# The order of TensorE's work in the first attention of a two-block kernel: pairs of heads taken two at a time

## The reference, cut to what matters

```python
s = einsum('bgrqd,bgkd->bgrqk', qb, kb) - slopes * dist      # 8 heads of 64, 2 groups of keys
pr = masked_softmax(s, valid)                                # causal
o_branch = einsum('bgrqk,bgkd->bgrqd', pr, vb)
...
gates = sigmoid(gate)                                        # one per token, head and branch
o = gates[..., 0:1] * o_cmp + gates[..., 1:2] * o_slc + gates[..., 2:3] * o_win
```

## Time and profile before

| | |
|---|---|
| median of three executions | 1574.64 us |
| the profiled execution, its own time | 1576.77 us |
| its span, first to last instruction | 1575.0 us |
| TensorE busy | 1518.0 us, 96% of the span |
| VectorE, ScalarE, GpSimd busy | 866.1, 640.2 and 218.4 us |
| mean granted TensorE clock | 0.98 of full |
| the first attention after its compressed scores | 284.6 to 364.2 us |

### The profile page before, as it was taken

One profiled execution on the slowest core, in us unless ns is written; L12 is line 12 of the kernel. 1 busy time (PEld: TensorE's weight loads), 2 busy tenths in 40 slices (PEclk: granted clock), 3 DMA queues, 4 the chain that ended last, 5 costly groups with the idle time before them and its releaser, 6 DMA issues. The chain is left out here.

```text
span 1575.0 us, 21715 instructions
## 1 busy us (share of the span) xinstructions
PE 1518.0 (96%) x8438; PEld 1241.9 (79%) x8438; DVE 866.1 (55%) x1296; ACT 640.2 (41%) x928; POOL 218.4 (14%) x195
## 2 busy tenths in 40 slices
PE   6998999999999899999999998999899999999997
PEld 5868988667888788888888876787578888888886
DVE  5755456773444477767743266798735444443223
ACT  5454432563323344444432245564644443442221
POOL 0005000781000000000000001189700000000000
PEclk9999999999999999999999999999989999999999
DMA  5210023001333312232233232122012332222221
GB/s 200 96 54 16 2 95 153 21 2 41 100 100 107 107 54 84 103 107 90 80 106 99 93 136 100 50 92 81 28 54 81 107 106 80 107 90 79 95 92 72
DMA packets 22535, 132.17 MB, mean 84 GB/s; under 512 B 2481, under 2 KB 2865, under 8 KB 12225
## 3 DMA queue, kind: packets, MB, share of 16 engines
q1 hardware_dynamic: 20672, 123.48, 22.8%
q0 software_dynamic: 928, 6.36, 1.1%
q10 hardware_dynamic: 864, 1.36, 0.2%
HBM read 129.09 MB, written 2.10 MB: 83 GB/s over the span
## 5 line engine op out<-in xcount | busy, mean ns | idle before, releaser
L322 PE MATMUL ps<-AH,whi 128*128 128x512 f32 x1280 | 507.3, 396 | 22.6 <-DVE wlo L2309 12.3
L323 PE MATMUL ps<-AL,whi 128*128 128x512 f32 x1280 | 503.3, 393 | 0.0
L324 PE MATMUL ps<-AH,wlo 128*128 128x512 f32 x1280 | 502.8, 393 | 0.0
L309 DVE TENSOR_TENSOR wlo<-raw,whi 128x2048 fp32r<-128x2048 f32 (+3 forms) x124 | 253.1, 2041 | 264.5 <-ACT whi L302 264.1
L322 PEld LDWEIGHTS ps<-AH,whi 128*128 128x128 f32 x1280 | 243.7, 190 | 77.4 <-issue 20.1
L302 ACT ACTIVATE whi<-raw 128x2048 fp32r<-128x2048 f32 (+3 forms) x124 | 210.3, 1696 | 183.6 <-PE ps L324 183.6
L324 PEld LDWEIGHTS ps<-AH,wlo 128*128 128x128 f32 x1280 | 243.3, 190 | 51.9
L323 PEld LDWEIGHTS ps<-AL,whi 128*128 128x128 f32 x1280 | 243.7, 190 | 49.9
L322 PE MATMUL ps<-HH,whi 128*128 128x512 f32 x352 | 136.9, 389 | 0.0
L323 PE MATMUL ps<-HL,whi 128*128 128x512 f32 x352 | 136.9, 389 | 0.0
L324 PE MATMUL ps<-HH,wlo 128*128 128x512 f32 x352 | 136.9, 389 | 0.0
(11 more groups left out here) (384 smaller groups left out, 1925.1 us busy)
## 6 DMA issues: line engine op xcount, KB each, us to landing
raw<-wstream SPq DMA_DIRECT2D x78, 1024.0 KB, 4.8
raw<-wstream SPq DMA_DIRECT2D x32, 704.0 KB, 4.2
raw<-wstream SPq DMA_DIRECT2D x16, 768.0 KB, 4.3
hT<-xT SPq DMA_DIRECT2D x4, 512.0 KB, 7.8
raw<-wstream SPq DMA_DIRECT2D x4, 512.0 KB, 3.7
W1k<-w1k_d POOLq DMA_DIRECT2D x1, 2048.0 KB, 9.1
W1v<-w1v_d POOLq DMA_DIRECT2D x1, 2048.0 KB, 15.4
BT<-bias_d POOLq DMA_DIRECT2D x1, 1024.0 KB, 5.5
```

The source lines that it names most:

```text
L309: nc.vector.tensor_tensor(WL[b][:, 0:n], RAW[b][:, 0:n], WH[b][:, 0:n].bitcast(F32), ALU.subtract).then_inc(w_lo_done, 1)
L322: nc.tensor.matmul(out_, WH[b][:, w], xh[:, k, :], start=start and k == 0, stop=False)
L323: nc.tensor.matmul(out_, WH[b][:, w], xl[:, k, :], start=False, stop=False)
L324: last = nc.tensor.matmul(out_, WL[b][:, w], xh[:, k, :], start=False, stop=stop and k == n - 1)
```

## The change

Only TensorE's order changes; every product, transpose and wait inside `scores`, `turn`, `values` and the compressed helpers stays, and the lists of the other engines stay as they are. The loop now runs over k = 0 to 16. A step takes turn(2k), values(2k-2), values(2k-1), turn(2k+1), scores(2k+3), scores(2k+4). The compressed products come behind the values and ahead of a turn (k = 4, 7, 11, 15), the compressed turns behind turn(7) and behind scores(10). `mix_gate(0, 0)` is still ahead of the last values.

```diff
@@ -1318,25 +1318,30 @@
             scores(2)
             pe.wait_ge(kv_c_sb, 1)
             compressed_scores()
-            for i in ITER:
-                if 2 < i < len(PAIRS):
-                    scores(i)
-                if i - 2 < len(PAIRS):
-                    turn(i - 2)
-                if i >= 3:
-                    values(i - 3)
-                if i == 8:
+            last = len(PAIRS) // 2
+            for k in range(last + 1):
+                if k < last:
+                    turn(2 * k)
+                if k:
+                    values(2 * k - 2)
+                    if k == last:
+                        mix_gate(pe, 0, 0)
+                    values(2 * k - 1)
+                if k == PER_QT // 2:
+                    compressed_values(0).then_inc(acc_ps, 1)
+                if k > PER_QT // 2 and k % 4 == 3:
+                    compressed_values((k + 1) // 4 - 1)
+                if k < last:
+                    turn(2 * k + 1)
+                if k == 3:
                     pe.wait_ge(cs_pr, 1)
                     compressed_turn(0)
-                if i == 9:
+                for i in (2 * k + 3, 2 * k + 4):
+                    if i < len(PAIRS):
+                        scores(i)
+                if k == 3:
                     pe.wait_ge(cp_sb, 1)
                     compressed_turn(1)
-                if i == PER_QT + 2:
-                    compressed_values(0).then_inc(acc_ps, 1)
-                if i > PER_QT + 2 and i % PER_QT == 1:
-                    compressed_values(i // PER_QT - 1)
-                if i == len(PAIRS) + 1:
-                    mix_gate(pe, 0, 0)
```

## The result

The kernel after the change takes **1589.84 us** (median of 4 runs, 1589.79 to 1593.55) against 1573.39 for the kernel before (4 runs, 1570.18 to 1576.15): a ratio of 1.0111, interval 1.0093 to 1.0129, or 16.5 us more. The forecast was 1588, slower, with a range of 1582 to 1595.

What follows compares the result with a forecast made beforehand. TensorE was taken to bound the kernel, busy 1518.0 of 1575.0 us. Stretch terms of +12.3 and +1.7 for the clock made +14.0 on the median of 1574.64: 1588.6, put at 1588 us, range 1582 to 1595.

Steps and rivals of the forecast that it cites:

- The bound and the direction: Whole kernel: TensorE's queue bounds it, and the new order makes it slower, at a chance of 0.91.
- the scaling road: Odd pair in the attention: scores, softmax chain, two GpSimd scalings, half turn, next odd scores; 7.7 us at 512 columns.
- The prices of a step: Two pairs in the attention: chain, two scalings, release, half turn; 7.7, 6.4, 5.1, 3.8 us at 512, 384, 256, 128.
- The step that failed: VectorE and ScalarE queues: nothing there ends later than GpSimd's scaling of the odd pair, so no time was added.
- The sign named in the prediction: TensorE's turns: idle time ahead of them put down to GpSimd grows to over 20 us, about 1.8 per double step.
- The cover of the compressed products: Scores 11 to 25: compressed products cost nothing, as TensorE has 1.8 us to spare per cycle; without cover 0.9 each.
- The end: From scores(31) to the mix stage: 4.1 us for 6.59, a change of -2.5 us.
- The start: Ahead of scores(3): turn(1) now comes first, with turns at the low clock; +1.8 us.
- The stretch of 512 columns: Scores 3 to 9: three cycles of 7.7 plus 1.4 for the compressed softmax, 24.6 us for 21.92, +2.7.
- The clock term: Last two cycles and end of the attention run at 1.2 GHz: +1.7 us, bounds 0 and +9.
- The rival of the saved changes: Attention: fewer TensorE mode changes decide, up to 6.4 us saved, 1568.2; chance 0.04 for faster, 0.05 for the same.
- The wide loss of clock: Rival: low clock from the 384-column pairs on, +22 us, 1597; chance 0.07.

Runs made afterwards that it cites:

- e4: Kernel after the change, with scores issued one pair earlier, so one more double step lies between an odd pair's scores and its turn: 1575.47 us, ratio 1.0011.
- e12: Kernel after the change, with copies of turned pairs ahead of minima and exponentials in every step, GpSimd's scaling left full: 1592.54 us, ratio 1.0129.
- e2: Kernel after the change, with GpSimd scaling only the first 128 columns of each head's probabilities (output not the reference's): 1589.13 us, ratio 1.0096.
- e1: Kernel after the change, with copies of turned pairs ahead of minima (VectorE) and exponentials (ScalarE) in odd steps only: 1585.71 us, ratio 1.0070.
- e6: Kernel before the change, with only the compressed products and compressed turns moved next to a turn: 1574.80 us, ratio 1.0007.
- e8: Kernel before the change, with GpSimd scaling only the first 128 columns of each head's probabilities (output not the reference's): 1572.08 us, ratio 0.9980.
- e5: Kernel before the change, still one pair at a time, with scores moved to the end of each step, behind turn and values: 1647.99 us, ratio 1.0476.

## Why the prediction was right, and where not

**The bound and the direction** held: the order of TensorE's queue turned a hidden chain into a cycle, and TensorE, which had stood as full in the earlier trace rows, stands idle ahead of the turns. e4 confirms it by giving back the distance, and e12 shows the scaling road alone with 16.6 us of waits.

**The prices of a step** held. Forecast 7.7, 6.4, 5.1, 3.8; measured in steady steps 7.69, 6.33, 5.02, 3.76. The terms were all from rows: chain, two scalings, release, half turn. e12 shows that the scaling road makes these steps by itself. GpSimd's gap ahead of the odd pair, forecast at about 1.3, is 0.88 in the step shown.

**The step that failed** is the one on the other engines' queues: "I find nothing that ends later", because "the copies of turned probabilities are done before that scaling is". Taken by itself the reason is true, 330.95 and 331.00 against 331.39. It leaves out what still follows each. The copies stand behind minima and exponentials of the newest scores, start 1.94 and 2.73 us after those scores at 384 columns (327.54 and 328.33 less 325.60), and through the even turn, the products and one more copy they hold the whole next odd turn until 331.10. Alone, that road makes 6.27 (e2) where the scaling makes 6.33 (e12): it does not end later, it ends as late. The sign named in the prediction, over 20 us put down to GpSimd, came out as 20.5 us with 0.9 of it put down to GpSimd. And the four distances, though forecast rightly, did not prove the scaling road: e2 has nearly the same ones with most of the scaling gone.

**The cover of the compressed products** failed with it. That "TensorE has 1.8 us to spare in a cycle" was true, but its spare time lay ahead of the even turn, and the product stands on the copy road, behind the products and ahead of the odd turn. It cost 7.01 - 6.33 = 0.7 and 5.58 - 5.02 = 0.6, not 0. e1 removes just that.

**The end** was forecast at 4.1 us and took 6.82. The term counted the road of pair 31 and left out the last compressed product, 2.08 us at the low clock, and the turn of pair 30 that waits 0.93 for its copy. In e1, also at the low clock there, the end takes 5.36. This is 2.7 us, the largest miss of any term.

**The start** gave +0.6, not +1.8. The term rested on turns at the low clock; in this execution the clock was high there (mean 1.00 from 278 to 286.5 us, 0.89 before). That fall is in some executions of these kernels and not in others, so it was not the change's to have. It also makes the +0.6 too small: e6 and e8, whose TensorE order is still that of before here, take 5.57 and 5.58 us at full clock for the 6.44 of before, and against them the change costs 1.4.

**The stretch of 512 columns** took 1.3 us more than forecast, all in its last step, 10.09. Half of TensorE's clock went there for 3.37 us, worth 3.37 - 3.37 / 1.8 = 1.5 by the earlier trace rows. **The clock term** of +1.7 was half right in its place. The forecast let the last two cycles and the end, from 363.7 us, run at 1.2 GHz; the clock was low from 369.9 on only, and in addition at 305.0. What it cost at the end no run separates from the rest, so whether 1.7 was the right size stays open. The reading behind it was also a little off: the earlier trace rows has 1.00 at 384 and 256 columns, but 0.96 at 512.

**The rival of the saved changes** fell to the distance, as the prediction said; its own price was too high as well (0.14 per double step at 512 for 0.34). The wide loss of clock did not come with this change. It exists: e5, in which TensorE waits far more, has a mean of 0.54 over its last 56 us.

The misses by stretch, -1.2, +1.3, -0.4, +0.5, +0.5, +0.3 and +2.7, add up to +3.7; with the 1.7 for the clock, which was forecast by itself, the attention came out 2.0 us over the +14.0. The forecast of 1588 was 1.8 us low. Part of that nearness is luck. The forecast started from 1574.64, and the kernel before then ran at 1573.39; by differences it is 16.5 us for 14.0. And the misses of the start and of the 512 columns, one from a fall of the clock in the profile of before, one from a fall in that of after, nearly cancel.

## What to carry to other kernels

When groups of work on an in-order queue are made larger, count for each pair what still lies between its producer and its consumer; the shortest distance sets the step, not the mean. Then walk every other queue by the same count, copies included: a copy that stands behind the newest scores' work is as late as that work, even if its own input has long been there. And where removing one suspected wait gives nothing, take it away together with the next one before it is acquitted: here 0.7 us for one (which can't be told from nothing), 4.1 for the other, 7.0 for both. A step of the forecast length is no proof either, as long as another road can make the same length.

## What the runs showed of the hardware

The clock fell inside a wide stretch, right behind a single wait. TensorE in the kernel after, timeline, then busy time in the two windows around the fall:

```profile
301.01 1.77 PE L1238 MATMUL ps<-KT,QT 64*128 64x512 f32 x8
305.03 1.94 PE L329 MATMUL ps<-ident,PR 128*128 128x128 f32 x8 [2.25 <-ACT PT L1352]
306.90 2.69 PE L1265 MATMUL ps<-PT,V 128*64 128x128 f32 x32
```

```profile
301.01:305.03 4.02, 1.77 (x10) 0.72 (x9) 3.03 (x10) 2.07 (x6) 3.12 (x3) 1.00 0.00 0
305.03:308.40 3.37, 3.37 (x22) 3.04 (x24) 0.95 (x4) 1.58 (x5) 3.10 (x2) 0.50 0.02 5
```

At 305.03 it goes from 2.4 to 1.2 GHz, after a wait of 2.25 us, and eight transposes take 1.94 where they took 1.06 at 309.67. The Trainium skill, page "TensorE: Matmul & The Clock Gate", section "Why this matters for your kernels", warns of long idle gaps between bursts. Whether 2.25 us is long the runs leave open. A wait of 2.03 us at 289.23, in the same kernel, brought no fall; the same wait of 2.25 in e2 was followed by a mean clock of 0.62 (304.06 to 308.50); and in e12 the clock fell at 334.5 after waits of 1.04 and 0.67 us. Nor did a long wait stand ahead of the fall at the end of the kernel before, where the gaps are 0.15 us. So the length of one wait alone does not decide it. What the fall costs here is the 1.5 us estimated above.

Products with V of two pairs in a row save nothing, 2.11 against 2 x 1.03, while scores in a row save 0.2 (1.92 against 2 x 1.06). A saved change of mode was thus worth something for one group and nothing for the other.
